# Two transformer layers on one core: three down sweeps partly whole, and the context pass of four products in step

## The reference

```python
ada = lambda t, g, shift, scale: rms_norm(t, g) * (1 + scale) + shift
ffn = lambda t, pre: (silu(t @ w_gate) * (t @ w_up)) @ w_down      # inner width 2816
x = x + 0.5 * m(2) * ffn(ada(x, norm_ffn1, m(0), m(1)), 'ffn1')    # the same for the context xc
y, yc = token_mix(ada(x, norm_mix, m(3), m(4)), ...)               # four mixers from one projection
x = x + m(5) * y                                                   # output projection inside y
x = x + 0.5 * m(8) * ffn(ada(x, norm_ffn2, m(6), m(7)), 'ffn2')
```

## Time and profile before

| | |
|---|---|
| median of three runs | 2187.9 us (2187.58 to 2188.36) |
| the profiled execution | 2188.3 us, its span 2186.5 us |
| TensorE matmul busy | 2146.8 us, 98% |
| VectorE, ScalarE, GpSimd busy | 66%, 47%, 28% |
| chain that ended last | TensorE 90%, VectorE 5%, ScalarE 2% |

### The profile page before, as it was taken

One profiled execution on the slowest core, in us unless ns is written; L12 is line 12 of the kernel. 1 busy time (PEld: TensorE's weight loads), 2 busy tenths in 40 slices (PEclk: granted clock), 3 DMA queues, 4 the chain that ended last, 5 costly groups with the idle time before them and its releaser, 6 DMA issues.

```text
span 2186.5 us, 32383 instructions
## 1 busy us (share of the span) xinstructions
PE 2146.8 (98%) x12181; PEld 1793.6 (82%) x12181; DVE 1447.5 (66%) x2042; ACT 1022.0 (47%) x1621; POOL 616.9 (28%) x615
## 2 busy tenths in 40 slices
PE   7999999999999999999999999999999999999998
PEld 4888878987766778987888898888889887889997
DVE  4887887775577456876676784445448858776555
ACT  4544445554455543553344453222235556645444
POOL 0566566402000036344444420000003201261000
PEclk9999999999999999999999999999999999999999
DMA  9476675633343354745545464444546445576564
GB/s 305 149 221 189 171 216 162 177 94 90 97 116 88 90 171 130 207 143 162 155 147 175 128 197 145 145 142 148 153 125 165 116 121 153 152 206 175 184 187 135
DMA packets 471966, 340.64 MB, mean 156 GB/s; under 512 B 13226, under 2 KB 437654, under 8 KB 471686
## 3 DMA queue, kind: packets, MB, share of 16 engines
q1 hardware_dynamic: 441312, 238.06, 37.6%
q0 software_dynamic: 29056, 96.35, 15.1%
q10 hardware_dynamic: 1446, 4.19, 0.5%
HBM read 326.96 MB, written 12.36 MB: 155 GB/s over the span
## 4 chain that ended last, share of the span: by engine, by line
PE 90%; DVE 5%; ACT 2%; issue 2%; DMA 1%; POOL 0%; SPq 0%; DVEq 0%; ACTq 0%; POOLq 0%
PE bank L832 20%; PE bank L833 20%; PE bank L837 19%; PE bank L900 4%; PE bank L910 4%; PE bank L901 3%; PE bank L984 2%; PE bank L990 2%; PE bank L985 2%; DVE w_lo L801 1%; PE bank L1358 1%; PE bank L1334 1%; PE bank L1125 1%; PE bank L1132 1%; PE bank L1126 1%
## 5 line engine op out<-in xcount | busy, mean ns | idle before, releaser
L801 DVE TENSOR_TENSOR w_lo<-raw,w_hi 128x1024 fp32r<-128x1024 f32 (+1 forms) x442 | 583.5, 1322 | 527.3 <-PE bank L837 312.6
L791 ACT ACTIVATE w_hi<-raw 128x1024 fp32r<-128x1024 f32 (+1 forms) x442 | 461.7, 1045 | 621.3 <-PE bank L833 289.2
L832 PE MATMUL bank<-h_hi,w_hi 128*128 128x512 f32 (+1 forms) x1728 | 601.5, 360 | 2.7 <-DVE X L2047 1.5
L833 PE MATMUL bank<-h_lo,w_hi 128*128 128x512 f32 (+1 forms) x1728 | 592.5, 355 | 0.0
L832 PEld LDWEIGHTS bank<-h_hi,w_hi 128*128 128x128 f32 x1728 | 326.5, 189 | 58.9 <-issue 11.8
L837 PE MATMUL bank<-h_hi,w_lo 128*128 128x512 f32 (+1 forms) x1728 | 367.1, 355 | 0.0
L833 PEld LDWEIGHTS bank<-h_lo,w_hi 128*128 128x128 f32 x1728 | 326.7, 189 | 45.4 <-issue 1.0
L837 PEld LDWEIGHTS bank<-h_hi,w_lo 128*128 128x128 f32 x1728 | 291.5, 189 | 45.5
L832 PE MATMUL bank<-inner_hi,w_hi 128*128 128x256 f32 (+1 forms) x654 | 206.2, 337 | 0.0
L833 PE MATMUL bank<-inner_lo,w_hi 128*128 128x256 f32 (+1 forms) x654 | 203.3, 332 | 0.0
L2470 POOL DMA_DIRECT2D wm<-in_w_mod_dram x128 | 92.6, 724 | 362.0 <-DVE gstage L2031 159.3
(11 more groups left out here) (305 smaller groups left out, 3483.3 us busy)
## 6 DMA issues: line engine op xcount, KB each, us to landing
wm<-in_w_mod_dram POOLq DMA_DIRECT2D x128, 512.0 KB, 4.0
raw<-in_w_in_dram SPq DMA_DIRECT2D x108, 512.0 KB, 3.9
raw<-in_ffn_w_down_dram SPq DMA_DIRECT2D x94, 512.0 KB, 3.9
raw<-in_ffn_w_gate_dram SPq DMA_DIRECT2D x88, 512.0 KB, 4.1
raw<-in_ffn_w_up_dram SPq DMA_DIRECT2D x88, 512.0 KB, 4.0
raw<-in_w_out_dram SPq DMA_DIRECT2D x24, 512.0 KB, 4.1
raw<-in_ffn_w_down_dram SPq DMA_DIRECT2D x24, 384.0 KB, 3.9
raw<-in_w_branch_dram SPq DMA_DIRECT2D x16, 512.0 KB, 4.6
```

The source lines that it names most:

```text
L791: act.activation(w_hi[w_slot[n]][:, 0:unit.rows, :], raw[unit.slot][:, 0:unit.rows, :], ACT.Copy).then_inc(hi_made, 1)
L801: dve.tensor_tensor(w_lo[w_slot[n]][:, 0:unit.rows, :], raw[unit.slot][:, 0:unit.rows, :], w_hi[w_slot[n]][:, 0:unit.rows, :].bitcast(F32) ...
L832: pe.matmul(psum, w_hi[s][:, k, :], hi, start=(k == 0), stop=False)
L833: mm = pe.matmul(psum, w_hi[s][:, k, :], lo, start=False, stop=False)
```

## The change

Three of the four halved sweeps (the output projection stays as it is) do their first three blocks for both streams at once, and only the last five in halves: 3 + 5 + 5 = 13 steps instead of 16. Their last inner chunk is no longer made in halves. The squares and their sums of the first three blocks are 512 columns wide. The norm of stream 0 still begins at step 8, so that blocks 0 to 4 are made beside steps 8 to 12, and 5 to 7 after the sweep. In every quad with both streams the pass over stream 1 takes all four products in step, the third and fourth two blocks behind.

```diff
+WHOLE_STEPS = 3
+def whole_steps(l, name):
+    if (l, name) not in HALVED:
+        return DC
+    return 0 if name == "out" else WHOLE_STEPS
+def step_block(l, name, i):
+    return i if i < DC else i - DC + whole_steps(l, name)
+def step_streams(l, name, i):
+    whole = whole_steps(l, name)
+    return range(2) if i < whole else range(i // DC, i // DC + 1)
...
-    return (l, (ffn, part)) in HALVED and j == 2 * PARTS[part][1] - 1
+    return whole_steps(l, (ffn, part)) == 0 and j == 2 * PARTS[part][1] - 1
...
-    return PARTS[name[1]][1] if by_tokens(l, name) else DC * sweep_halves(l, name)
+    return PARTS[name[1]][1] if by_tokens(l, name) else 2 * DC - whole_steps(l, name)
...
+            def sweep_loads(l, name, u0):
+                return [(u0, 0)] if (l, name) not in HALVED else [(u0, 0), (u0 + DC, whole_steps(l, name))]
...
-                        for again in range(sweep_halves(l, (ffn, part))):
-                            stage(first["down", l, ffn, part] + again * DC, DC, lambda j: [((0, n), columns(wd, l, j * P, n, c0))])
+                        for u0, block in sweep_loads(l, (ffn, part), first["down", l, ffn, part]):
+                            stage(u0, DC - block, lambda j: [((0, n), columns(wd, l, (j + block) * P, n, c0))])
...
                 for st in streams(n):
                     last = st == streams(n)[-1]
-                    if key == (0, 1) and st == 0:
+                    if last and n == TOK or key == (0, 1):
                         pe.wait_ge(lo_made, units[u0].product + 1)
-                        pair_pass(range(u0, u0 + 4), st, last, bank[0:4], (0, 2, 4, 6), key)
+                        pair_pass(range(u0, u0 + 4), st, last, bank[0:4], (0, 0, 2, 2) if last else (0, 2, 4, 6), key)
                         continue
...
-                        square(key, d % DC, d // DC)
+                        square(key, step_block(l, name, d), step_streams(l, name, d) if halved else streams(n)[-1:])
...
+                if halved:
+                    for k in range(sweep_steps(l, name) - DC, DC):
+                        norm_hi(key, k, 0)
...
                 if halved:
-                    norm_lo(key, DC - 1, 0)
+                    for k in range(sweep_steps(l, name) - DC, DC + 1):
+                        if k < DC:
+                            norm_scale(key, k, 0)
+                        norm_lo(key, k - 1, 0)
...
+                whole = whole_steps(l, name) if (l, name) in HALVED else 0
+                for k in range(1, whole):
+                    squares.wait(pool, (key, k, 1))
+                    if k > 1:
+                        pooled.wait(pool, (key, k - 1, 1))
+                    before = wa[:, 0, :] if k == 1 else wb[:, 1, :]
+                    pooled.done(pool.tensor_tensor(wb[:, 1, :], before, wa[:, k % 2, :], ALU.add), (key, k, 0))
+                    pooled.mark((key, k, 1))
                 for st in streams(n):
                     squares.wait(pool, (key, 0, st))
-                    for k in range(1, DC - 1):
+                    for k in range(max(whole, 1), DC - 1):
```

More of the change, by code:

```diff
@@ L189 @@
 HALVED = [(0, (1, 2)), (0, "out"), (0, (2, 2)), (1, (1, 2))]
-def sweep_halves(l, name):
-    return 2 if (l, name) in HALVED else 1
+WHOLE_STEPS = 3
[8 more added lines that the diff above has]
+    return range(2) if i < whole else range(i // DC, i // DC + 1)
 def by_tokens(l, name):
@@ L655, in stream_cols, with step_cols @@
             return slice(st * LAT, (st + 1) * LAT)
+        def step_cols(l, name, i, n):
+            if (l, name) not in HALVED:
+                return slice(0, n)
+            sts = step_streams(l, name, i)
+            return slice(sts[0] * LAT, (sts[-1] + 1) * LAT)
         def next_modulation(l, name, d):
@@ L748, in _ @@
                                  ((0, DC), w_branch[l].rearrange("k (c p) n -> p (k c) n", p=P)[:, :, d * P:(d + 1) * P]))
-                        for again in range(sweep_halves(l, "out")):
-                            stage(first["out", l] + again * DC, DC, lambda j: [((0, DC), columns(w_out, l, j * P))])
+                        for u0, block in sweep_loads(l, "out", first["out", l]):
+                            stage(u0, DC - block, lambda j: [((0, DC), columns(w_out, l, (j + block) * P))])
                     for part, (c0, n) in enumerate(PARTS):
@@ L1159, in down @@
                         pe.wait_ge(added, a0 + d - 1)
-                    cols = stream_cols(d // DC) if (l, (ffn, part)) in HALVED else slice(0, n)
+                    cols = step_cols(l, (ffn, part), d, n)
                     def inner_rhs(k):
@@ L1164, in inner_ready @@
                     def inner_ready(k):
-                        if k == rows - 1 and (l, (ffn, part)) in HALVED:
+                        if k == rows - 1 and whole_steps(l, (ffn, part)) == 0:
                             half_lo.wait(pe, (l, ffn, part))
@@ L1438, in _ @@
                     pe.wait_ge(added, a0 + d - 1)
-                    cols = stream_cols(d // DC) if (l, "out") in HALVED else slice(0, n)
+                    cols = step_cols(l, "out", d, n)
                     if (l, "out") in HALVED and d == DC:
@@ L1467, in _, with square @@
         def _(act):
-            def square(key, k, st):
+            def square(key, k, sts):
                 if k >= 2:
-                    pooled.wait(act, (key, max(k - 2, 1), st))
-                squares.done(act.activation(wa[:, k % 2, stream_cols(st)], X[:, k, stream_cols(st)], ACT.Square), (key, k, st))
+                    pooled.wait(act, (key, max(k - 2, 1), sts[-1]))
+                cols = slice(sts[0] * LAT, (sts[-1] + 1) * LAT)
+                squares.done(act.activation(wa[:, k % 2, cols], X[:, k, cols], ACT.Square), (key, k, sts[0]))
+                squares.mark((key, k, sts[-1]))
             def square_start(k):
@@ L2045, in add_block @@
                     dve.wait_ge(unit_done, u0 + d + 1)
[L2046 to L2049, removed]
+                    block = step_block(l, name, d)
+                    for st in step_streams(l, name, d) if halved else streams(n):
+                        ins = dve.scalar_tensor_tensor(out=X[:, block, stream_cols(st)], in0=bank[4 + d % 2][:, stream_cols(st)],
+                                                       scalar=gatev[:, gate_i, block, st:st + 1],
+                                                       in1=X[:, block, stream_cols(st)], op0=ALU.mult, op1=ALU.add)
                     ins.then_inc(added, 1)
```

## The result

| | before | after |
|---|---|---|
| median of six runs | 2188.4 us (2187.6 to 2189.8) | 2199.9 us (2198.1 to 2201.1) |
| profiled execution, its span | 2188.3 us, 2186.5 us | 2200.8 us, 2199.1 us |
| granted clock, mean | 0.998 | 0.995 |
| TensorE matmul busy | 2146.8 us | 2152.1 us |

The ratio after to before is 1.0051, with a 95% interval of 1.0041 to 1.0061: the kernel is slower by 11.5 us. The forecast was slower by 9.1.

What follows compares the result with a forecast made beforehand. TensorE, busy 98% of the span, was taken as the bound. The terms -2.3 + 3.9 + 6.3 + 1.2 gave +9.1 us, 2197.0 us against the median; range 2189.3 to 2201.

Steps and rivals of the forecast that it cites:

- Whole products: Three down sweeps: blocks 0 to 2 as one 512-column product instead of two of 256, 0.77 us saved a sweep, 2.3 in all.
- 0.41 of waiting: First product of each halved sweep: its wait for the last inner chunk, 0.41 us, was taken to go with whole products.
- sweep B: Down sweep of layer 0's second feed-forward, one of three changed; forecast 0.77 us shorter.
- The late norm: Quads (four products) after the three sweeps: TensorE waits 0.9 us for block 4, then 0.1 to 0.3 a block; 3.9 us in all.
- The late release: Five quads: first weights released 4.28 us later, delaying ScalarE's split for the fifth product and its queue; 6.3 us in all.
- Rival 1: ScalarE's and VectorE's queue behind the fifth product's split: release shift isn't passed on; 2185.6 or 2189.5 us; chance 15%.
- near 5 us: Opening of layer 0: sign that TensorE waits near 5 us for the seventh product's split, with granted clock 0.5 after it.
- The clock: Opening of layer 0: the 4.3 us wait brings one fall to the half clock, costing 1.2 us.
- Rival 2: Opening of layer 0: no fall of the clock, all else as forecast, 2195.8 us; chance 10%.
- Rival 4: Three late norms: the clock falls there too, 3 x 1.2 us more, 2200.6 us; chance 10%.
- Rival 3: VectorE's modulation accumulates at the opening of layer 0 get cheaper in the shift, also avoiding the clock fall: 2192.7 us; chance 10%.

Runs made afterwards that it cites:

- the run with later pieces: Changed kernel with modulation pieces, sums, copies and turns of the first seven groups two units later at the opening of layer 0: 2193.3 us, ratio 1.0021.
- the run with filler: Changed kernel with 9 identity products that nothing reads put ahead of the seventh product at the opening of layer 0: 2197.5 us, ratio 1.0042.
- the first experiment: Changed kernel with the context pass in pairs again, the three sweeps staying at 13 steps: 2191.1 us, ratio 1.0012.
- the last run: One whole step, context pass in pairs, modulation pieces and sums at the opening of layer 0 two units later: 2186.1 us, ratio 0.9988 to the kernel before.
- both fillers: Changed kernel with 18 or 9 unread identity products ahead of the seventh product at the opening of layer 0: 2201.7 us and 2197.5 us.

## Why the prediction held

Forecast +9.1, measured +11.5 in the medians and +12.6 in the profiled span. By its own steps:

- **Whole products, -2.3 us.** Measured -1.9. Whole products run at 5.57, as priced. The first product's 0.41 of waiting was the loose term: in sweep B a part of it stayed (-0.49 instead of -0.77).
- **The late norm, +3.9.** Measured +4.15. The mechanism is right, its place off by a block: I looked at block 4, behind the sum of squares, and missed that the low row of block 3 also comes late, behind the sweep's last split and the scale of block 4. VectorE's order from there on is as I counted it (block 4's low row ends 3.04 us behind the quad's start, 3.07 by the forecast), and so the loss is too. That it comes from the number of whole steps is shown by the runs with none, one and four.
- **The late release, +6.3.** Measured 0.68 and 3.5 at the opening of layer 0 (4.3 forecast), 1.45 (1.3) and 1.06 (0.7) at the two others, 0 at the mixers: 6.7. The shift of the release against TensorE was 4.29, and 4.28 was forecast. The 1.06 is 0.80 in the run without whole steps, so 0.26 of it comes only where the quad is late as well. Rival 1, that the shift be taken up, is out: both ends of the chain moved alike. The forecast's sign of "near 5 us" of waiting for the seventh split didn't fit its own sum, which had 0.6 + 4.3 - 0.65 there; it was 4.10. But the chain was not rigid, as the run with later pieces shows.
- **The clock, +1.2.** This is the term of the sum that was mis-sized. One fall, as forecast, right behind the long wait; but I took its price from the earlier trace rows as it stood, 3.0 us of work under the half clock with matmuls of 256 columns. Here TensorE worked 5.0 us under it (84.42 to about 89.4), with matmuls of 512 columns. By an estimate at the rate of the earlier trace rows, 1.2 of 3.0 us lost, 5.0 us cost 2.0; the shape gives the other 0.3, since a 512-column matmul takes 0.43 instead of 0.23 and a 256-column one 0.20 instead of 0.12. So the length of the stretch was the larger part of the error. At the opening the fall is 2.3 us by the trace and 2.4 by the run with filler; in the run without whole steps TensorE worked 5.6 us under it, and the stage is 2.8 longer than the wait explains. Rival 2, no fall, is out. Rival 4 (falls at the three late norms) didn't come; with four whole steps one of them did. A further fall, of 1.0 us, came late in layer 1's mixers, far behind the last wait that the change made longer. TensorE after, and then before, at about this place:

```profile
1966.72 0.55 PE L890 MATMUL bank<-h_hi,w_hi 128*128 128x256 f32 x1 [1.90 <-issue]
```
```profile
1954.88 0.36 PE L863 MATMUL bank<-h_hi,w_hi 128*128 128x256 f32 x1 [1.58 <-issue]
```

  and this is the window behind it, after:

```profile
1966.80:1970.30 3.50, 3.50 (x17) 3.50 (x18) 2.88 (x6) 1.93 (x4) 1.17 (x2) 0.52 0.36 107
```

  The longer wait alone doesn't explain it. In the first experiment the same wait is 1.86 us, and TensorE goes on at full clock:

```profile
1957.79 0.36 PE L890 MATMUL bank<-h_hi,w_hi 128*128 128x256 f32 x1 [1.86 <-issue]
```
```profile
1957.90:1961.40 3.50, 3.50 (x30) 3.50 (x31) 2.88 (x6) 1.95 (x4) 1.15 (x2) 1.00 0.34 102
```

  It is 1.89 with one whole step and 1.94 in the last run, also without a fall, and the five other kernels with the same pass in step have 1.57 to 1.60 and none. In the same way the 2.8 us wait ahead of the last stage's quad, which is in every kernel, is followed by the half clock in eight of the twelve profiled executions and not in the other four (pieces later, one whole step, both fillers). These four spend 0.7 to 0.9 us less there; it isn't 1.2, because TensorE at full clock then waits 0.4 to 0.5 us for rows. So no run ties the 1.0 us to the change, and what decides whether such a wait brings a fall stays open. The six times of the kernel after lie in two groups, 2198.1 to 2199.0 with a mean granted clock of 0.997 and 2200.8 to 2201.1 with 0.995 to 0.996, and the profiled execution is of the second. Falls that come in some executions only fit this; which ones a shorter execution lacks no profile shows.
- **Rival 3, cheaper accumulates.** Out: the four of the chain kept their 0.74, 1.67, 1.60 and 1.97 us, and GpSimd's first addition moved along, from 65.85 to 70.40. In the Trainium skill, the page "SBUF — State Buffer", section "Who interferes with whom", says that such operations of VectorE and GpSimd shut one another out; long rows are what one would then expect of neighbours that move together. Which of the two holds the other no run here shows.

In the profiled span the forecast is short by 3.5 us: the price of the fall 1.1, the second fall 1.0, the releases 0.4, the sweeps 0.4, the norms 0.25, and 0.25 ahead of the opening quad. In the medians it is short by 2.4.

The Trainium skill's page "TensorE: Matmul & The Clock Gate", Part 1, has the halved clock as the default, from which activity releases the engine. This case's traces agree: 0.50 behind the 4.1 us wait with TensorE idle (12 matmuls in 4.9 us), 1.00 behind the same wait with TensorE at work in it (23).

## What to carry to other kernels

Reordering the work of a saturated engine changes when it lets go of its inputs: for each buffer ask for the last use, not for the total, and follow the released instruction's whole queue to the engine's next demand. A norm or any other chain that runs beside a loop needs the loop's steps as cover, so shortening the loop uncovers it: shorten by as many steps as the chain has to spare, here one, and no more. Price a fall of the clock by how long TensorE works under it and by the shape of the matmuls that it does there, and when a producer is moved, move its consumer too.

## What was new about the hardware

- The half clock's price goes with the work done under it: 1.2 us lost in 3.0 us of 256-column matmuls (0.20 us each against 0.12), 2.2 in 4.9 of 512-column ones (0.43 against 0.23).
- The length of one wait doesn't tell whether the clock falls behind it. 4.1 us with the engine idle brought the fall in both kernels that had it, and 5.7 us in a third. But 1.90 did and 1.86, 1.89, 1.94 and 2.03 didn't; 2.8 us did in eight executions of twelve; 1.17 and 0.37 close together did in one quad and not in two others of the same kernel.
- Where TensorE has waits to spare, a fall can cost nothing: between 41 and 50 us the granted clock was 0.81 before and 1.00 with one whole step, and the opening quad takes 27.0 us in both. With a longer stretch, 0.73 there in the last run, it takes 28.6.
- Whole products of the down sweeps run at 5.57 us and the up products of the earlier trace rows at 5.44, with operands of the same shape and no waits. The cause wasn't tried and stays open.
- A 256-column matmul on plain float32 operands came out as two of 0.21 us each, almost as long as a 512-column one of the other kind.
